# Two-block network on one core: half of a layer's modulation blocks, and the second gate, summed on VectorE along the free axis

## What is computed

```python
for l in range(2):
    sh_l, sc_l, g_l = jnp.split(jax.nn.silu(c) @ w_mod[l] + b_mod[l], 3, axis=-1)
    sh_c, sc_c, g_c = jnp.split(jax.nn.silu(c_ctx) @ w_mod[l] + b_mod[l], 3, axis=-1)
    hl = xl * (1.0 + sc_l) + sh_l
    hc = xc * (1.0 + sc_c) + sh_c
    parts_l = jnp.split(hl @ w_in[l], SPLIT_POINTS, axis=-1)
    ...
    xl = _layernorm(DEEPNORM_ALPHA * xl + g_l * out_l, ln_g[l], ln_b[l])
    if not last:
        xc = _layernorm(DEEPNORM_ALPHA * xc + g_c * out_c, ln_g[l], ln_b[l])
```

## Time and profile before

| | us |
|---|---|
| median of three runs (2924.89 to 2925.16) | 2925.16 |
| the profiled execution's own time | 2924.98 |
| its span, first to last instruction | 2923.2 |
| TensorE matmul, busy | 2897.2 (99%) |
| VectorE, busy | 1730.2 (59%) |
| ScalarE, busy | 1330.8 (46%) |
| GpSimd, busy | 100.3 (3%) |
| bytes moved | 527.49 MB, mean 180 GB/s |
| granted TensorE clock, mean | 0.998 of full |

### The profile page before, as it was taken

One profiled execution on the slowest core, in us unless ns is written; L12 is line 12 of the kernel. 1 busy time (PEld: TensorE's weight loads), 2 busy tenths in 40 slices (PEclk: granted clock), 3 DMA queues, 4 the chain that ended last, 5 costly groups with the idle time before them and its releaser, 6 DMA issues.

```text
span 2923.2 us, 42667 instructions
## 1 busy us (share of the span) xinstructions
PE 2897.2 (99%) x15914; PEld 2410.9 (82%) x15914; DVE 1730.2 (59%) x2954; ACT 1330.8 (46%) x2045; POOL 100.3 (3%) x162
## 2 busy tenths in 40 slices
PE   8999999999999999999999999999999999999998
PEld 6777777777788788888887888888888888888887
DVE  3344443434577736666885566667876556565566
ACT  2433333323433535544555545455655445354455
POOL 0000010101000001111000000000000000000000
PEclk9999999999999999999999999999999999999999
DMA  9844343434365324444544444444555555555555
GB/s 380 352 184 162 148 170 145 165 153 169 141 226 213 130 101 148 142 144 145 183 151 166 173 173 159 173 160 172 187 187 202 187 187 190 198 185 190 187 200 188
DMA packets 76378, 527.49 MB, mean 180 GB/s; under 512 B 8864, under 2 KB 11168, under 8 KB 13632
## 3 DMA queue, kind: packets, MB, share of 16 engines
q1 hardware_dynamic: 72448, 513.83, 47.5%
q0 software_dynamic: 2912, 9.57, 0.9%
q10 hardware_dynamic: 864, 1.94, 0.2%
HBM read 523.22 MB, written 2.10 MB: 180 GB/s over the span
## 4 chain that ended last, share of the span: by engine, by line
PE 96%; DVE 1%; DMA 1%; ACT 1%; issue 1%; POOL 0%; POOLq 0%; ACTq 0%; DVEq 0%; SPq 0%
PE bank L1906 27%; PE bank L1909 14%; PE bank L1896 9%; PE bank L1898 9%; PE bank L1897 9%; PE bank L2316 4%; PE bank L2315 4%; PE bank L2317 4%; PE bank L1942 2%; PE bank L1943 2%; PE bank L1944 2%; PE bank L1955 2%; PE bank L2124 1%; DMA raw<-stream 1%; PE bank L2083 1%; PE bank L2008 1%
## 5 line engine op out<-in xcount | busy, mean ns | idle before, releaser
L1123 DVE TENSOR_TENSOR w_lo<-raw,w_hi 128x1024 fp32r<-128x1024 f32 x784 | 949.6, 1225 | 616.7 <-ACT w_hi L616 613.8
L616 ACT ACTIVATE w_hi<-raw 128x1024 fp32r<-128x1024 f32 x784 | 824.2, 1057 | 725.3 <-DMA raw<-stream 286.1
L1896 PE MATMUL bank<-x,w_hi 128*128 128x512 f32 x1120 | 442.5, 395 | 1.2 <-DVE x L1205 1.2
L1898 PE MATMUL bank<-x,w_lo 128*128 128x512 f32 x1120 | 436.4, 390 | 0.0
L1897 PE MATMUL bank<-x,w_hi 128*128 128x512 f32 x1120 | 436.2, 389 | 0.0
L629 ACT ACTIVATE z<-bank 128x512 f32<-128x512 f32 x256 | 153.2, 598 | 461.4 <-PE bank L1909 307.5
L1906 PE MATMUL bank<-xs,w_hi 128*128 128x512 f32 x1184 | 304.7, 397 | 0.0
L1896 PEld LDWEIGHTS bank<-x,w_hi 128*128 128x128 f32 x1120 | 210.2, 188 | 84.2 <-issue 40.9
L1906 PE MATMUL bank<-mlp_x,w_hi 128*128 128x512 f32 x1024 | 257.1, 393 | 0.0
L1898 PEld LDWEIGHTS bank<-x,w_lo 128*128 128x128 f32 x1120 | 210.2, 188 | 44.7
L1906 PEld LDWEIGHTS bank<-xs,w_hi 128*128 128x128 f32 x1184 | 213.0, 189 | 39.9 <-DVE xs L1205 1.1
(11 more groups left out here) (341 smaller groups left out, 3510.2 us busy)
## 6 DMA issues: line engine op xcount, KB each, us to landing
raw<-stream SPq DMA_DIRECT2D x488, 1024.0 KB, 4.8
res<-tokens POOLq DMA_DIRECT2D x8, 512.0 KB, 8.9
work<-tokens POOLq DMA_DIRECT2D x16, 256.0 KB, 3.0
out<-res SPq DMA_DIRECT2D x8, 256.0 KB, 2.4
gain_sb<-final_gain ACTq DMA_DIRECT2D x1, 1024.0 KB, 7.5
table_sb<-tables ACTq DMA_DIRECT2D x1, 640.0 KB, 3.5
pool_sb<-pool_w POOLq DMA_DIRECT2D x8, 64.0 KB, 4.2
work<-lam_in POOLq DMA_DIRECT2D x1, 256.0 KB, 9.4
```

The source lines that it names most:

```text
L616: own.inc(act.activation(w_hi[:, 2 * unit.parity + g, :], raw[:, unit.slot, g * HALF:(g + 1) * HALF], ACT.Copy), hi_done, 2 * unit.number ...
L1123: own.inc(dve.tensor_tensor(w_lo[:, n, :], raw[:, unit.slot, g * HALF:(g + 1) * HALF], w_hi[:, n, :].bitcast(F32), ALU.subtract), lo_done, ...
L1896: pe.matmul(bank[:, :], hi, tile(k)[:, 0, :], start=k == 0, stop=False)
L1898: ins = pe.matmul(bank[:, :], lo, tile(k)[:, 0, :], start=False, stop=k == KT - 1)
```

## The change

- 24 of the 48 blocks beside the first layer's slots stay on TensorE (`BESIDE_PE`), in two turns of 12 instead of three of 16. The other 24 (`BESIDE_DVE`) hold the second layer's scale columns and the end of its shift in another layout: 128 output columns lie on the partitions and 512 rows of the matrix along the free axis, four tiles to a block. VectorE multiplies such a tile by a row with 512 values of the condition, the same on all partitions, and the instruction writes the sum besides the product (`accum_out`): eight instructions a block, for four tiles and two sides (`share_products`). The block of unit n is taken after VectorE's slot n - 2.
- The condition rows are made by DMA: `cond_sb` is written to a buffer in DRAM once, and read back to all partitions, 512 values a side at a time, into the last two tiles of `res` (four times two loads of 256 KB), all in SyncE's queue.
- The second gate's 16 blocks are laid out the same way, all 2048 rows along the free axis: one instruction of 128x2048 a block, with the condition in `gate_row` (one load of 1 MB into `work`). It is called after the slot instead of before it, and blocks 14 and 15 come together after slot 14.
- The sums over rows with ones, the copy and the collecting at the norm are gone; two short products (`stay_awake`) are in their place. `x_res` moves to `a_t` and `se`.

```diff
+TURN_ENDS = [40, 59]
+BESIDE_PE = [12, 13, 14, 16, 17, 21, 22, 28, 29, 33, 34, 40, 41, 45, 46, *range(51, 60)]
+BESIDE_DVE = [n for n in range(PAIRED, PAIRS) if n not in BESIDE_PE]
+ROWS = len(BESIDE_DVE) // 4
...
-    return 2 * u - (20 if u < GATED else 19)
+    if u < GATED:
+        return 2 * (BESIDE_PE + BESIDE_DVE)[u - 32] + 20
+    return 2 * u - 19
...
                 if before in mod_at and mod_at[before] >= GATED:
                     sp.wait_ge(gate_used, mod_at[before] - GATED + 1)
+                elif before in mod_at and mod_at[before] >= SUMMED:
+                    done = mod_at[before] - SUMMED + 1
+                    if done % ROWS == 0 and done < 4 * ROWS:
+                        sp.wait_ge(row_used, done // ROWS)
+                        load_row(0, done // ROWS)
+                    sp.wait_ge(share_used, done)
+                    if done % ROWS == 0 and done < 4 * ROWS:
+                        load_row(1, done // ROWS)
...
-            def gate_products(k):
+            def gate_product(k):
...
-                for j in range(4):
-                    w = raw[:, place % RAW_SLOTS, WIDE * j:WIDE * (j + 1)]
-                    c = cond_x[:, 4 * q + j, 2 * (SHARE - 1):2 * SHARE - 1]
-                    if q + j == 0:
-                        last = dve.tensor_scalar(gate_acc[group], w, c, None, ALU.mult)
-                    else:
-                        own.wait_own()
-                        last = stt_i(gate_acc[group], w, c, gate_acc[group], ALU.mult, ALU.add)
...
+                w = raw[:, place % RAW_SLOTS, :]
+                own.inc(dve.scalar_tensor_tensor(out=w, in0=w, scalar=1.0, in1=gate_row, op0=ALU.mult, op1=ALU.mult,
+                                                 accum_out=mod[:, GATED + k, 0:1]), gate_used, k + 1)
...
+            def share_products(d):
...
+                for s in range(2):
+                    for j in range(4):
+                        if s or j:
+                            own.wait_own()
+                        last = dve.scalar_tensor_tensor(out=z[:, 1, :], in0=raw[:, place % RAW_SLOTS, WIDE * j:WIDE * (j + 1)],
+                                                        scalar=1.0, in1=cond_row[s], op0=ALU.mult, op1=ALU.mult,
+                                                        accum_out=part[:, j, s:s + 1])
...
                     slot(unit, epilogue, before, after, between=first_tiles, late=l == 1, tail=tail)
+                    if l == 0 and unit.fixed + 2 in BESIDE_DVE:
+                        share_products(BESIDE_DVE.index(unit.fixed + 2))
...
-                    if l == 0:
-                        gate_products(k)
                     slot(Unit([W_OUT0, W_OUT1][l] + k), residual(l, k, k % 2, k // 2 + 1), before, after,
                          apart=l == 1 and k == KT - 1)
+                    if l == 0 and k < KT - 1:
+                        gate_product(k)
+                    if l == 0 and k == KT - 2:
+                        gate_product(KT - 1)
...
             def mod_beside(n):
 
-                if n < PAIRED:
+                if n not in BESIDE_PE:
                     return None
...
-                if l == 0:
-                    pe.wait_ge(gate_used, KT)
-                    pe.wait_ge(z_full, Unit(W_OUT0 + 14).taken + 1)
-                    for g in range(SHARE):
-                        window = slice(2 * (SHARE - 1 - g), 2 * (SHARE - 1 - g) + SQUARE)
-                        ins = pe.matmul(gemm_bank[0][SQUARE * g:SQUARE * (g + 1), :], gate_ones[:, window], gate_acc[g],
-                                        start=True, stop=True)
-                    ins.then_inc(gate_sum, 1)
-                else:
-                    stay_awake(att[5], 2)
+                stay_awake(att[5], 2)
```

More of the change, by code:

```diff
@@ L45 @@
 SHARE = 4
-TURNS = 19
+BESIDE = 3
+TURNS = KT + 2
+SUMMED = 56
 GATED = 80
@@ L243, in two_blocks @@
         chooser = place("chooser", [2 * SHARE])
-        gate_ones = place("gate_ones", [SQUARE + 2 * (SHARE - 1)])
         tiny = place("tiny", [64])
@@ L261, in two_blocks @@
         mix_rms = tiny[:, 56:58]
+        part = place("part", [4, 2])
+        rows_dram = nc.dram_tensor("cond_rows", (2, P, KT), F32, kind="Internal").ap()
+        cond_row = [res[:, KT - 2 + s, :] for s in range(2)]
+        flat_cond = cond_sb[:].rearrange("p k s -> p (k s)").rearrange("p (s k) -> p s k", s=2)
         top = tiny[:, 16:24]
@@ L280, in two_blocks @@
         h_tmp = [work[:, 0, :], work[:, 1, :]]
-        x_res = [work[:, 2, :], work[:, 3, :]]
+        x_res = [a_t[:, 0, :], se[:]]
+        gate_row = work[:, 0:4, :].rearrange("p n t -> p (n t)")
         total = work[:, 4, :]
@@ L821, in after @@
                                 late_tile(k)
-                    if l == 0 and (unit.fixed - PAIRED) % 16 == 15 and s != 3:
-                        take_mod(KT + (unit.fixed - PAIRED) // 16, 1, 1)
+                    if l == 0 and unit.fixed in TURN_ENDS:
+                        act.wait_ge(share_used, sum(n < unit.fixed for n in BESIDE_DVE))
+                        take_mod(KT + TURN_ENDS.index(unit.fixed), 1, 1)
                     def rest_of_operand():
@@ new lines, in share_products @@
+            def share_products(d):
+                place, q, m = mod_place(SUMMED + d), d // ROWS, SUMMED + 4 * (d % ROWS)
+                dve.wait_ge(raw_full[place % RAW_SLOTS], 16 * (place // RAW_SLOTS + 1))
+                if d % ROWS == 0:
+                    dve.wait_ge(rows_in, 32 * (q + 1))
+                own.wait_own()
+                for s in range(2):
+                    for j in range(4):
+                        if s or j:
+                            own.wait_own()
+                        last = dve.scalar_tensor_tensor(out=z[:, 1, :], in0=raw[:, place % RAW_SLOTS, WIDE * j:WIDE * (j + 1)],
+                                                        scalar=1.0, in1=cond_row[s], op0=ALU.mult, op1=ALU.mult,
+                                                        accum_out=part[:, j, s:s + 1])
+                        if s == 0 and j == 3 and d % ROWS == ROWS - 1:
+                            own.inc(last, row_used, q + 1)
+                        elif s == 0 or j < 3:
+                            own.inc_own(last)
+                own.inc(last, share_used, d + 1)
+                own.wait_own()
+                for s in range(2):
+                    target = mod[:, m:m + 4, s]
+                    start = vec[:, VEC_COLS["b_mod"] + m:VEC_COLS["b_mod"] + m + 4] if q == 0 else target
+                    tt(target, part[:, :, s], start, ALU.add)
@@ L1554, in norm @@
                         split(Unit(W_IN1 + 3))
-                        modulation(TURNS, 0, [(GATED, 0, SHARE, 0, 4)])
+                        gate, bias = mod[:, GATED:MODS, 0], VEC_COLS["b_mod"] + GATED
+                        tt(gate, gate, vec[:, bias:bias + KT], ALU.add)
                     if l == 1 and k in (3, 5):
```

74 lines of the change are left out of this document (40 added, 34 removed).

## The result

The changed kernel takes 2990.09 us, median of four runs (2988.0 to 2991.71); the kernel before, beside it, 2925.07. The ratio is 1.0222, 95% interval 1.0204 to 1.024. The forecast was 2989 us, within 2954 to 3022. The changed kernel's profiled execution is the slowest of its four, 2991.71 us with a span of 2990.0, so the profiles differ by 66.8 us where the medians differ by 65.0.

A forecast was written before the change was run, and what follows sets the result against it. TensorE, carrying 96% of the last-ending chain, was taken to bound the kernel. 2924.98 - 18.3 (input stage) + 80.8 (output-stage loop, chance 0.72) + 2 (clock at the norm) = 2989.5, so 2989 us, range 2954 to 3022.

The forecast's parts named there:

- Part 1: Input stage: 24 modulation blocks and one of three turns of column sums leave TensorE, saving 18.3 us (15 to 20).
- With no wait on w_lo: Sign to look for in the changed profile: in the input stage TensorE never waits on w_lo.
- VectorE's block: Input stage: a moved block costs VectorE about 7.2 us (6.4 to 8), eight products with sums and two small additions.
- I book it at nothing: Input stage: VectorE's 173 us more cost no time, covered by the two units of lead that w_lo has.
- Part 2: First output product: gate blocks one slot later close a loop through SyncE's loads; the stage ends 80.8 us later.
- the turn: Output stage: load pair 7.35, rounding 1.06, then VectorE's 2.15, 3.29 and 2.45; 16.3 us a unit against TensorE's 10.88.
- Part 3: Norm: removing the sums gives nothing; TensorE's idle time of some 20 us lowers its clock, costing 2 us (0 to 6).
- Their removal is worth nothing: Norm: the gate's sums and column sums on TensorE lay inside other waits, so dropping them saves 0 us.
- The first (no loop): Output stage: the loop does not close, only the input stage's saving counts; 2907 us, chance 0.06.
- The second (a milder loop): Output stage: the gate load ahead costs nothing, weights land in 4.8 us, 13.75 us a unit; 2954 us, chance 0.10.
- The third (sums at half rate): VectorE: products writing a sum take 1.03 ns more per element; about 3025 us, chance 0.12.
- The fourth: Input stage: VectorE falls behind or the change saves little; 5 to 15 us on the forecast, no chance given.

The follow-up runs named there:

- the variant put back: The changed kernel with VectorE taking each gate block ahead of its slot again, as before the change; 2906.69 us, ratio 0.9932 to the kernel before.

## Why the prediction was right, step by step

**Part 1.** Forecast 18.3 us, measured 19.6, inside 15 to 20. The mechanism held at every boundary, and two prices were off. Of the twelve behind attention products the six behind scores lost 1.00 us as priced (3.77 to 2.77 us), but the six behind products with V lost 1.17 (3.99 to 2.82), 1.0 us more in all. The six behind a turned output lost 0.63 as priced, the six behind nothing 0.19 instead of 0.25, and the turn of column sums was 0.95. That makes 18.9 us; the last 0.7 are spread over the slots at less than 0.1 us each. "With no wait on w_lo" stands too, since all twelve waits ended with the copy.

**VectorE's block.** Forecast 7.2 us with 6.4 as the lower bound; measured 6.04 us from the first product to the w_lo behind it (183.30 to 189.34). The term that was off is the start-to-start time: I took 0.78 us from old blocks that read their own result back, and added 0.06 for the sum; a product with its sum takes 0.73, since the 0.08 us of reading ends where the next starts. The error lay on the safe side, and it mattered more than I said: with 9.1 us a block the stage is 31 us longer. "I book it at nothing: the cover is the two units of lead" is right for 6 us; at 7.2 it would by my estimate, a line from 0 to 31 us over 2.9 us a block, have cost some 12 us. Where that line bends was not tried, so this cost is not shown. That the booking held is thus in part luck: the block came out 1.2 us shorter than priced, and at the priced length nothing was measured.

**Part 2.** All terms of the turn hold: 7.34 for the pair, 1.09 from rounding to w_lo, 5.31 from the first w_lo to the gate block, 2.29 for the block. Two turns of the changed kernel were longer, 18.45 at unit 8 with ScalarE waiting 15.2 us for the load, and 17.1 with the folding. The load's scatter was not in my sum (with no turn like that at unit 8 the stage took 253.2 us, in the first profile with small products before the norm). The terms on VectorE came out 0.3 us a turn below theirs, which happened to make up for it: the stage is 1.9 us shorter than forecast. Undoing the place, and separately SyncE's order, removed the loop; moving the old block made it.

**Part 3.** "Their removal is worth nothing" stands within a microsecond or two: the versions without the sums and without idle time had 11.8 us at the norm in two profiles and 13.4 or 13.5 in four, the kernel before 10.6 and 11.8, and no median tells them apart. The clock was mis-sized within its range: 5.7 us against a forecast of 2, and 4.4 against the second profile of before. Small products in the wait gave back 4.3 us of it in one profile and 1.1 in another.

**The rivals.** The first (no loop) is refuted by the changed profile and priced by the variant put back, 2906.7 us against my 2907. The second (a milder loop) is wrong because the gate's load ahead does cost 2.0 us; without it the kernel takes 2960. The third (sums at half rate) is refuted: 128x512 with a sum takes 692 ns against 693 without, and 128x2048 takes 2.28 us and 0.08 us for the reading, where half rate asked for 4.4. The Trainium skill, "Vector Engine (DVE) Microarchitecture Reference", section "Points that are easy to get wrong", says that the two sources take both read ports and leave none for reading back the accumulator, and that this halves the rate; these rows, with two sources in SBUF and a sum read back, disagree, and the measurement decides. The fourth did not happen with blocks of 6 us; with blocks of 9 us it did.

**What stays open.** The start took 136.4 to 142.2 us in sixteen profiles, with TensorE waiting for loads while the DMA engines were at mostly 0.9 to 1.0 of their time; neither the write of the condition nor the kernel version accounts for it, and what does was not found. The difference of 1.5 us in the rest scatters likewise and goes with the clock in the second layer's norm: below 1.00 for 10 us there in the first profile of before (1942.4 us), never in that of the gate block put back (1939.7). Whether the bare norm costs one or two microseconds is below what was measured.

## What to carry to other kernels

Before a step is moved past another on an engine, write down which ring place it frees, which load waits for that place, what is queued behind that load, and whether the next thing on the same engine needs it: if it does, the transfer's full time enters every turn, here 7.3 of 16 us. Such a loop can be opened on either side, by the engine's order or by the queue's. And when a change has a good part and a bad one, time the parts alone: the moved blocks were worth some 19 us (2906.7 against 2925 to 2927), hidden under a move that cost 79.

## What the runs showed of the hardware

- Two loads of 1 MB issued 0.4 us apart landed so that the second was usable 7.3 us after their release; one such load behind a 32 KB one was usable after 5.3 us.
- A VectorE product that writes its sum costs no more than one without: 692 ns at 128x512 and 2.28 us at 128x2048, with a separate record of 0.08 us for the reading.
- A wait can be put down to the wrong engine when two semaphores are waited for: four waits of TensorE named w_lo, and each ended 0.10 us behind ScalarE's copy.
- TensorE's granted clock fell to 0.50 (the level of 1.2 GHz, against 2.4 at 1.00) in the norm even without idle time before it, once in two profiles of the unchanged kernel and in every variant's. Behind 4.7 to 22 us of idle time it stood at 0.50 from the means' first product on, and the norm took 16.2 to 16.7 us; behind 2.6 us it was still at 1.00 there, fell within 2 us, and the norm took 15.15 us.
